# Another order and another spacing of the work that is laid between the steps of layer 0's attention

## The chip, the cores and the metric

The kernel runs on one core of one Trainium2 chip. The metric is the device time of one execution in microseconds (us). All arithmetic is in 32-bit floats.

## What is computed

The reference runs a first block of two layers and then a second block. The change touches layer 0 of the first block alone. Its parts that matter here are:

```python
shift, scale, gate = split(silu(c) @ w_ada[l] + b_ada[l], 3)       # the modulation, 6 x 512 columns of w_ada
h = x * (1 + scale) + shift                                        # 512 rows; the context's 256 rows likewise
(..., g_lat) = split(h @ w_in[l])                                  # the last 1024 columns of w_in are the gate
y_b = global_gqa(...)          # 4 heads, all keys
y_c = diff_attention(...)      # 4 heads, (softmax(q1 k1) - lam * softmax(q2 k2)) v
y_d = window_gqa_latent(...)   # 4 heads, keys within 128 positions, and the context
y = concatenate([y_a, y_b, y_c, y_d]) * silu(g_lat)
x_new = layer_norm(alpha * x + gate * (y @ w_out))
```

## The kernel before

The 512 + 256 rows stand as six tiles of 128 rows, four of the latent and two of the context (tiles 4 and 5). Five programs (one for each engine) are written out by hand, and each of them walks through the same steps in the same order; semaphores tie them together. The PSUM has eight banks of 128 x 512 floats.

**The attention of a layer** is `attend(l)`. In layer 0 it goes through 48 steps and four more that empty the pipeline, so i = 0 to 51. Steps 0 to 23 are the differential kind (c in the code: a tile and one of its four heads, with two score maps), 24 to 35 the global kind (b) and 36 to 47 the local kind (d), both with a tile and two heads a step. TensorE (PE) issues in step i: q, the transposes of a tile's queries, if step i + 2 starts a tile; S, the scores of step i (L973), into banks 2 to 5, which the two maps of every step share; t, the transposes of the softmax weights of step i - 2 (L988); V, the products with the values (L1007) of step i - 3, in the differential kind on even steps alone; o, the transposes of a finished tile's heads (L748), on odd steps. ScalarE (ACT) issues in a differential step: the copy of the first half of t out of its bank, the two exponentials of step i (L1571), and only then the copy of the second half of t. VectorE (DVE) issues the row maxima of step i (L2141), the settling of step i - 1 and, in the later kinds, its share of the copies. S of step i + 1 writes where the exponentials of step i have read.

q, t and o use banks 6 and 7 in turn, by a place that `turn_banks` works out. `open_bank(b)` makes PE wait until the last user of a bank has been read out.

**The work laid between the steps** is the generator `gate_and_ada(l)` of each engine, and `alongside` spreads it evenly over the 52 steps. It has 40 pieces in layer 0: first 24 pieces G, each two products of 128 x 512 of the gate's second half (`product_pieces`, L799), four to a tile, into bank 0, the fourth followed by ACT's copy (`gate`); then eight parts of the modulation (`ada`, `later_ada`: parts 4 and 5 of layer 0 and all six of layer 1), each of two pieces. The first, P, is eight products of 32 rows x 512 columns into bank 0 (L761), which ACT copies to a row in SBUF. The second, T, is four transposes of that row (L748) into bank 6 + n % 2, where n is the part's number in its layer; T opens that bank first, whoever used it last. DVE then reduces the bank (L1958) and adds the bias (L1960):

```python
bank_free(0, [ada_act.at("row", l, n)])
yield True
b = 6 + n % 2
open_bank(b)
pe.wait_ge(*ada_act.at("row", l, n))
transposes(raw[n % 2], 4, b).then_inc(turn_done(("ada", l, n)), 1)
```

A piece is issued after all that its step issues. With P and T numbered 0 to 7, the even spacing puts G on steps 0 to 29 (12 of them on steps 0 to 14, and 12 on steps 15 to 29), P0 on step 31, T0 on 32, P1 on 33, T1 on 35, P2 on 36, T2 on 37, P3 on 39, T3 on 40, P4 on 41, T4 on 42, P5 on 44, T5 on 45, P6 on 46, T6 on 48, P7 on 49 and T7 on 50. After step 51 comes the first tile of y, then a barrier of the engines and the layer's end, which needs the gate of all tiles and the modulation.

**Weights** come through a ring of six slots of 512 KB (`list_weights`, `Weights`). SyncE's queue (SP) issues the loads in the order of the list, each after the products of the block six places ahead of it have ended. A part of the modulation takes four loads (32 for the eight parts), the gate's second half four, and the output projection eight.

Of the kernel before, what the change touches and what calls it, by code (L numbers as in the profile page):

```python
# [23 lines left out]
DEPTH = 2  # L24
# [118 lines left out]
        pass  # L143


def run(stream):
    for _ in stream:
        pass
# [18 lines left out]
def later_ada(l):  # L167

    return [(l, 4), (l, 5)] + [(l + 1, n) for n in range(6)]


def list_weights(ring, a):
    def rows(key, w, c0, n, per=2, moved=()):
        v = w.rearrange("(k p) n -> p k n", p=P)
        for i in range(KT // per):
            ring.add(key + (i,), v[:, per * i:per * i + per, c0:c0 + n], (per, n), i in moved)

    def cols(key, w, c0, split=False):
        v = w.rearrange("(k p) n -> p k n", p=P)
        ring.add(key, v[:, :, c0:c0 + P], (KT, P), split)  # L180

    def wide(key, w, k):
        ring.add(key, w[k * P:(k + 1) * P, :].rearrange("p (k n) -> p k n", k=1), (1, D), True)

    for n in range(4):
        rows(("ada", 0, n), a["w_ada"][0], 512 * n, 512)
    for l in range(DEPTH):
        w = a["w_in"][l]
        for t in range(2):
            tag, c = (("b", C_B), ("d", C_D))[t]  # L190
            rows((tag, l), w, c, 512)
            for name, c in (("q", C_AQ), ("f", C_FF), ("b", C_FB)):
                cols(("hg", l, t, name), w, c + P * t)
            if t == 0:
                rows(("ai", l), w, C_AI, 256)
                rows(("c", l), w, C_C, 512)
            else:
                rows(("cv", l), w, C_CV, 256)
        rows(("g0", l), w, C_G, 512)
        rows(("g1", l), w, C_G + 512, 512)  # L200
        if l < DEPTH - 1:
            for l_, n in later_ada(l):
                rows(("ada", l_, n), a["w_ada"][l_], 512 * n, 512)
        for n in range(2):
            rows(("out%d" % n, l), a["w_out"][l], 512 * n, 512, 2, MOVED[l, n])
    w = a["w_in_2"][0]
    for i, c in enumerate(FM2[2:]):
        cols(("fm", i + 2), w, c)
    rows(("gmlp", 2), w, 0, 512)
    for i, c in enumerate(FM2[:2]):  # L210
        cols(("fm", i), w, c)
    rows(("q", 2), w, 512, 256, 4)
    rows(("kv", 2), w, 1024, 512)

    def compression(i):
        v = a["nsa_cmp_w1_2"][0, i].rearrange("(k p) e -> p k e", p=P)
        for half in range(2):
            ring.add(("w1", i, half), v[:, 8 * half:8 * half + 8, :], (8, CMP_HID))

    compression(0)  # L220
    rows(("ng", 2), w, 1536, P, 8)
    compression(1)
    for d in range(KT):
        for n in range(4):
            cols(("gate", d, n), a["w_gate_2"][0], n * D + d * P, True)
        cols(("branch", d), a["w_branch_2"][0].rearrange("n c d -> (n c) d"), d * P, True)
    for k in range(KT):
        wide(("out2", k), a["w_out_2"][0], k)
    for f in range(FT):
        cols(("mlp1", f), a["w_mlp1_2"][0], f * P, True)  # L230
    for f in range(FT):
        wide(("mlp2", f), a["w_mlp2_2"][0], f)


def build(nc, a, out):
    ctx = ExitStack()
    with ctx:
# [313 lines left out]
        def attention_steps(l):  # L551

            out_ = []
            if l == 2:
                for m in range(LT):
                    for kind in BRANCHES:
                        for e in range(2):
                            out_.append((kind, m, e))
                return out_
            for kind in "cbd":  # L560
                for m in range(last_q_of(l)):
                    for e in range(4 if kind == "c" else 2):
                        out_.append((kind, m, e))
            return out_

        def window(kind, m):
            if kind == "cmp":
# [157 lines left out]
        def tensor_program(pe):  # L725
# [207 lines left out]
                    bank_free(0, [gate_act.at("row", tag, l, m)])  # L933

            def gate_and_ada(l):
                yield from gate(l, 1)
                if l < DEPTH - 1:
                    yield from ada(later_ada(l))

            def prepare(l, k, banks):  # L940
                kind, m, e = attention_steps(l)[k]
# [161 lines left out]
            def layer(l):  # L1103
                for t in range(2):
                    beside = stream(l, t)
                    for m in range(AHEAD):
                        if t == 0 and l == 0 and m + 2 < TT:
                            modulate(0, m + 2, stage_x[m + 2])
                        next(beside)
                        if t == 0 and l > 0 and m == 0:  # L1110
                            pe.wait_ge(*tail_dve.at("z", l - 1, TT - 1))
                            modulate(l, TT - 1, z[:, TT - 1, :])
                    scan_inputs(l, t)
                    next(beside)
                    alongside(scan(l, t), 14, beside, beside_steps(l, t))
                    stage_end(1 + 3 * l + t)
                alongside(attend(l), len(attention_steps(l)) + 4, gate_and_ada(l), 4 * last_q_of(l) + (16 if l < DEPTH - 1 else 0))
                turn_y(l, 0)
                stage_end(3 + 3 * l)
                layer_end(l)  # L1120
# [271 lines left out]
        def scalar_program(act):  # L1392
# [154 lines left out]
                    yield True  # L1547

            def gate_and_ada(l):
                yield from gate(l, 1)  # L1550
                if l < DEPTH - 1:
                    yield from ada(later_ada(l))

            def prepare(l, k, banks):
                kind, m, e = attention_steps(l)[k]
# [105 lines left out]
            def layer(l):  # L1661
                for t in range(2):
                    beside = stream(l, t)
                    for m in range(AHEAD):
                        if t == 0 and l == 0 and m + 2 < TT:
                            modulate(0, m + 2)
                        next(beside)
                    scan_inputs(l, t)
                    if t == 0:
                        act.wait_ge(*lam_dve.at("sums", l))  # L1670
                        act.activation(lam[:, 2:4], lam[:, 0:2], ACT.Exp).then_inc(lam_act(("exp", l)), 1)
                    next(beside)
                    alongside(scan(l, t), 14, beside, beside_steps(l, t))
                    stage_end(1 + 3 * l + t)
                alongside(attend(l), len(attention_steps(l)) + 4, gate_and_ada(l), 4 * last_q_of(l) + (16 if l < DEPTH - 1 else 0))
                stage_end(3 + 3 * l)
                layer_end(l)

# [236 lines left out]
        def vector_program(dve):  # L1915
# [169 lines left out]
                    yield True  # L2085

            def gate_and_ada(l):
                for _ in range(4 * last_q_of(l)):
                    yield True
                if l < DEPTH - 1:  # L2090
                    yield from ada(later_ada(l))

            def settle(l, k):
                kind, m, e = attention_steps(l)[k]
# [246 lines left out]
            def layer(l):  # L2341
                lam_init = 0.8 - 0.6 * math.exp(-0.3 * l)
                dve.wait_ge(*gains.at("all", l))
                dve.tensor_scalar(neg_sinks[:], sinks[:], -1.0, None, ALU.mult).then_inc(lam_dve(), 1)
                dve.tensor_tensor(lam_rows[:, 0::2, :], lam_rows[:, 0::2, :], lam_rows[:, 1::2, :], ALU.mult).then_inc(lam_dve(), 1)
                dve.wait_ge(*lam_dve.now())
                dve.reduce_sum(lam[:, 0:2], lam_rows[:, 0::2, :], AX).then_inc(lam_dve(("sums", l)), 1)
                for t in range(2):
                    beside = stream(l, t)
                    for m in range(AHEAD):  # L2350
                        if t == 0 and l == 0 and m + 2 < TT:
                            modulate(0, m + 2)
                        next(beside)
                    scan_inputs(l, t)
                    next(beside)
                    alongside(scan(l, t), 14, beside, beside_steps(l, t))
                    if t == 0:
                        dve.wait_ge(*lam_act.at("exp", l))
                        dve.tensor_tensor(lam[:, 4:5], lam[:, 3:4], lam[:, 2:3], ALU.subtract).then_inc(lam_dve(), 1)
                        dve.wait_ge(*lam_dve.now())  # L2360
                        dve.tensor_scalar(lam[:, 5:6], lam[:, 4:5], -lam_init, None, ALU.add).then_inc(lam_dve(("lam", l)), 1)
                    stage_end(1 + 3 * l + t)
                alongside(attend(l), len(attention_steps(l)) + 4, gate_and_ada(l), 4 * last_q_of(l) + (16 if l < DEPTH - 1 else 0))
                stage_end(3 + 3 * l)
                layer_end(l)

# [455 lines left out]
```

## Time and profile before

| | us |
|---|---|
| median of 3 runs | 2188.32 (2186.58 to 2189.64) |
| the profiled execution, its own time | 2191.96 |
| its span on the core | 2190.1 |
| PE busy in the span | 2054.4 (94%) |
| VectorE busy | 1154.3 (53%) |
| ScalarE busy | 783.3 (36%) |

The sum of a change is made against the profiled execution; the time outside its span is 1.9 us. Rows of the trace give the start in us from the span's start, a duration, the engine, the line, and, in brackets, how long the engine had been idle and what ended that. A product of 32-bit floats stands as two records, a transpose as one. The rows themselves stand below.

### The profile page before, as it was taken

To read this page: it belongs to the slowest core of one execution; us is meant where nothing else is said; L and a number is where in the kernel's file an instruction comes from. 1 tells how busy PE (TensorE), PEld (TensorE's weight loads), DVE (VectorE), ACT (ScalarE), POOL (GpSimd) and SP (SyncE) were. 2 spreads that over 40 slices of the span, in tenths; PEclk is the share of its full clock that TensorE was granted. 3 is DMA by queue.
4 is the path that set the end of the run, shared out by engine and by line. 5 is a ranking of instruction groups with operands and counts; after the bars stand their busy time and mean duration, and the time that the engine had idled before them with its cause. 6 is when DMAs were issued, how large, how long until landed. Compare 5 with 4: busy or idle time off the path is not lost.

```text
span 2190.1 us, 27157 instructions
## 1 busy us (share of the span) xinstructions
PE 2054.4 (94%) x10380; PEld 1445.3 (66%) x10380; DVE 1154.3 (53%) x2484; ACT 783.3 (36%) x1671; POOL 54.5 (2%) x96
## 2 busy tenths in 40 slices
PE   5989999999889999898998989999999999999999
PEld 2565465555547665564565677885788877888887
DVE  1655136555657848226467677977444435333333
ACT  2132123554453323233465524336422224223222
POOL 2000000000000000000000010000000000000000
PEclk9999999999889999999799999998999999999999
DMA  9111010001444211121000332221233332333331
GB/s 294 35 52 39 25 63 20 20 1 40 154 154 122 78 48 39 40 64 62 1 1 11 107 81 77 79 78 29 68 97 97 98 94 60 98 99 91 97 97 66
DMA packets 152687, 157.32 MB, mean 72 GB/s; under 512 B 5676, under 2 KB 114384, under 8 KB 152560
## 3 DMA queue, kind: packets, MB, share of 16 engines
q1 hardware_dynamic: 146672, 137.91, 20.7%
q0 software_dynamic: 5888, 17.68, 2.8%
q8 instruction: 84, 1.38, 0.3%
q14 instruction: 43, 0.35, 0.1%
HBM read 151.37 MB, written 4.19 MB: 71 GB/s over the span
## 4 chain that ended last, share of the span: by engine, by line
PE 73%; DVE 16%; ACT 5%; issue 3%; DMA 2%; POOL 1%; ACTq 0%; PEldq 0%; DVEq 0%; SPq 0%; PEld 0%; POOLq 0%
PE psum L787 11%; PE psum L1280 10%; PE psum L1281 9%; PE psum L1282 9%; PE psum L973 6%; PE psum L799 5%; PE psum L815 5%; PE psum L988 3%; PE psum L1007 3%; PE psum L748 2%; DVE arena L2430 2%; DVE stats L2141 1%; ACT arena L1394 1%; PE psum L833 1%; PE psum L761 1%
## 5 line engine op out<-in xcount | busy, mean ns | idle before, releaser
L1394 ACT ACTIVATE arena<-psum 128x384 f32<-128x384 f32 (+5 forms) x510 | 199.9, 420 | 626.7 <-PE psum L748 171.1
L1280 PE MATMUL psum<-part,part 128*128 128x512 f32 x992 | 387.7, 391 | 5.2 <-DVE part L2545 2.7
L1281 PE MATMUL psum<-part,part 128*128 128x512 f32 x992 | 387.4, 391 | 0.0
L1282 PE MATMUL psum<-part,part 128*128 128x512 f32 x992 | 387.3, 390 | 0.0
L787 PE MATMUL psum<-arena 128*128 128x512 f32 (+1 forms) x960 | 319.4, 488 | 0.8 <-ACTq L1397 0.8
L1394 ACT ACTIVATE part<-arena 128x1024 fp32r<-128x1024 f32 (+1 forms) x214 | 190.6, 924 | 226.3 <-PE psum L1282 150.0
L2545 DVE TENSOR_TENSOR part<-arena,part 128x1024 fp32r<-128x1024 f32 x112 | 137.1, 1226 | 252.1 <-ACT part L1394 252.1
L787 PEld LDWEIGHTS psum<-arena 128*128 128x128 f32 x960 | 178.9, 190 | 120.7 <-issue 105.7
L2141 DVE TENSOR_REDUCE stats<-psum 128x1 f32<-128x768 f32 (+6 forms) x208 | 139.0, 709 | 153.1 <-PE psum L973 151.6
L1280 PEld LDWEIGHTS psum<-part,part 128*128 128x128 f32 x992 | 186.6, 188 | 45.9 <-DVE part L2545 3.1
L1282 PEld LDWEIGHTS psum<-part,part 128*128 128x128 f32 x992 | 186.7, 188 | 39.3
L1281 PEld LDWEIGHTS psum<-part,part 128*128 128x128 f32 x992 | 186.6, 188 | 38.9
L799 PE MATMUL psum<-arena 128*128 128x512 f32 x320 | 157.7, 623 | 3.4 <-ACT arena L1394 3.4
L973 PE MATMUL psum<-arena 64*128 64x256 f32 (+6 forms) x672 | 152.2, 506 | 8.9 <-ACT arena L1571 7.8
L1571 ACT ACTIVATE arena<-psum,stats 128x768 f32<-128x768 f32 (+6 forms) x208 | 144.8, 702 | 41.4 <-DVE stats L2109 19.9
L988 PE MATMUL psum<-ident,arena 128*128 128x128 f32 (+1 forms) x672 | 117.3, 304 | 13.0 <-DVE arena L2155 9.0
L973 PEld LDWEIGHTS psum<-arena 64*128 64x128 f32 (+1 forms) x672 | 72.3, 199 | 82.6 <-issue 56.7
L815 PE MATMUL psum<-arena 128*128 128x512 f32 (+1 forms) x352 | 119.4, 501 | 0.0
L988 PEld LDWEIGHTS psum<-ident,arena 128*128 128x128 f32 (+1 forms) x672 | 77.5, 149 | 62.6 <-issue 37.9
L748 PE MATMUL psum<-ident,arena 128*128 128x128 f32 x456 | 76.7, 289 | 40.4 <-ACT arena L1394 16.8
L815 PEld LDWEIGHTS psum<-arena 128*128 128x128 f32 x352 | 67.2, 192 | 51.6 <-issue 47.6
L1007 PE MATMUL psum<-arena 128*64 128x128 f32 (+1 forms) x1344 | 101.0, 297 | 0.0
(279 smaller groups left out, 2358.7 us busy)
## 6 DMA issues: line engine op xcount, KB each, us to landing
arena<-in_w_in SPq DMA_DIRECT2D x75, 512.0 KB, 4.1
arena<-in_w_mlp SPq DMA_DIRECT2D x64, 512.0 KB, 3.8
arena<-in_w_ada SPq DMA_DIRECT2D x48, 512.0 KB, 5.3
arena<-in_w_gate SPq DMA_DIRECT2D x32, 512.0 KB, 4.0
arena<-in_w_out SPq DMA_DIRECT2D x24, 512.0 KB, 3.9
arena<-in_w_in SPq DMA_DIRECT2D x16, 256.0 KB, 3.3
arena<-in_w_branch SPq DMA_DIRECT2D x8, 512.0 KB, 3.7
arena<-in_x POOLq DMA_DIRECT2D x4, 512.0 KB, 9.1
```

Of the source, the lines that this page charges most:

```text
L787: mm = pe.matmul(bank(b)[:, c0:c1], lhs[:, k, m * P:(m + 1) * P], ring.view(tag, l, k // 2)[:, k % 2, c0:c1], start=k == 0, stop=k == kt - 1)
L799: mm = pe.matmul(bank(b), lhs[:, k, m * P:(m + 1) * P], ring.view(tag, l, k // 2)[:, k % 2, :], start=k == 0, stop=k == KT - 1)
L815: mm = pe.matmul(bank(b)[:, 0:t1 - t0], ring.view("hg", l, t, name)[:, k, :], h_t[:, k, t0:t1], start=k == 0, stop=k == KT - 1)
L973: mm = pe.matmul(score_map(l, k, j)[:, c0:c0 + rhs.shape[-1]], q[r0:r1, at_q:at_q + P], rhs[r0:r1, :], start=True, stop=True)
L988: mm = pe.transpose(bank(b)[0:w, x * P:(x + 1) * P], weights_of(l, k)[:, j, c0:c0 + w], ident[:])
L1007: mm = pe.matmul(bank(b)[64 * j:64 * j + 64, u * P:(u + 1) * P], value(kind, s, h), head_turned(l, k_, i)[0:w, x * P:(x + 1) * P], start=x ...
L1280: pe.matmul(dst, lo, x_hi_, start=first, stop=False)
L1281: pe.matmul(dst, hi, x_lo_, start=False, stop=False)
L1282: return pe.matmul(dst, hi, x_hi_, start=False, stop=last)
L1394: return act.activation(dst, src, ACT.Copy)
L1571: act.activation(weights_of(l, k)[:, j, lo:hi], score_map(l, k, j)[:, lo:hi], ACT.Exp, bias=col[:, j:j + 1], scale=1.0, accum_out=col[:, 2 ...
L2141: dve.reduce_max(col[:, j:j + 1], score_map(l, k, j)[:, lo:hi], AX, negate=True).then_inc(soft_dve(*names), 1)
```

## The change

The generator `gate_and_ada` gives the modulation's 16 pieces first and the gate's 24 after them, on PE, ACT and DVE. The gate's four loads stand behind the modulation's 32 in the list. And `paced` with a list of counts takes the place of `alongside`:

```diff
+def paced(main, filler, counts):
+    for _, n in zip(main, counts):
+        for _ in range(n):
+            next(filler)
+    for _ in filler:
+        pass
...
         rows(("g0", l), w, C_G, 512)
-        rows(("g1", l), w, C_G + 512, 512)
         if l < DEPTH - 1:
             for l_, n in later_ada(l):
                 rows(("ada", l_, n), a["w_ada"][l_], 512 * n, 512)
+        rows(("g1", l), w, C_G + 512, 512)
...
+        def pieces_beside(l):
+            n = len(attention_steps(l)) + 4
+            if l < DEPTH - 1:
+                parts_ = {0: 1, 1: 2, 2: 2, 3: 2, 5: 2, 7: 2, 9: 2, 11: 2, 13: 2}
+                pieces = {15, 17, 19, 21, 23, 25, 27, 29, 31, 33} | set(range(36, 49))
+                return [parts_.get(i, 1 if i in pieces else 0) for i in range(n)]
+            else:
+                total = 4 * last_q_of(l) + (16 if l < DEPTH - 1 else 0)
+                upto = [-(-i * total // n) for i in range(n + 1)]
+                return [upto[i + 1] - upto[i] for i in range(n)]
...
             def gate_and_ada(l):
-                yield from gate(l, 1)
                 if l < DEPTH - 1:
                     yield from ada(later_ada(l))
+                yield from gate(l, 1)
...
-                alongside(attend(l), len(attention_steps(l)) + 4, gate_and_ada(l), 4 * last_q_of(l) + (16 if l < DEPTH - 1 else 0))
+                paced(attend(l), gate_and_ada(l), pieces_beside(l))
```

So in layer 0: P0 on step 0; T0 and P1 on step 1; T1 and P2 on 2; T2 and P3 on 3; then T3 and P4 on 5, T4 and P5 on 7, T5 and P6 on 9, T6 and P7 on 11, T7 and the first G on 13. The other 23 G: one on each odd step from 15 to 33 (ten), and one on each of steps 36 to 48 (thirteen). For layer 1 the counts are those of the even spacing. The bank of each T, and its user before, by `turn_banks`: T0 bank 6, the queries' transposes; T2 bank 6, the first half of t of its own step; T1, T3, T4, T5, T6 and T7 the bank of the second half of t of their own step.

## Rows read from the trace of the kernel before

**Rows 1.** Busy time by stretch: length, engines (instructions), PE clock, DMA share, GB/s

```profile
391.70:413.80 22.10, 22.10 (x101) 11.05 (x101) 13.71 (x22) 11.51 (x26) 0.00 (x0) 0.92 0.06 22
413.80:463.10 49.30, 48.80 (x304) 28.65 (x302) 32.62 (x53) 30.01 (x70) 0.00 (x0) 1.00 0.00 1
463.10:496.70 33.60, 32.36 (x175) 16.91 (x174) 17.11 (x48) 16.50 (x54) 0.00 (x0) 0.95 0.01 1
496.70:565.20 68.50, 64.70 (x488) 39.88 (x486) 41.39 (x99) 33.61 (x83) 0.00 (x0) 0.95 0.28 93
565.20:637.40 72.20, 60.51 (x444) 35.16 (x442) 44.78 (x148) 33.65 (x101) 0.00 (x0) 0.86 0.34 118
```

**Rows 2.** Timeline of PE: the scores of steps 5, 8, 9 and 15

```profile
413.76 2.18 PE L973 MATMUL psum<-arena 32*128 32x512 f32 x8
...
429.19 1.56 PE L973 MATMUL psum<-arena 32*128 32x512 f32 x8
...
432.95 2.37 PE L973 MATMUL psum<-arena 32*128 32x512 f32 x8
...
463.11 1.56 PE L973 MATMUL psum<-arena 32*128 32x512 f32 x8
```

**Rows 3.** Timeline of step 3: scores, the second exponential, then ACT's two copies

```profile
405.27 1.92 PE L973 MATMUL psum<-arena 32*128 32x512 f32 x8
...
408.97 0.90 ACT L1571 ACTIVATE arena<-psum,stats 128x768 f32<-128x768 f32 x1
...
409.84 0.99 ACT L1394 ACTIVATE arena<-psum 128x384 f32<-128x384 f32 x2
```

**Rows 4.** Timeline of PE: a G and a P

```profile
446.69 1.88 PE L799 MATMUL psum<-arena 128*128 128x512 f32 x4
...
544.98 1.92 PE L761 MATMUL psum<-arena,csil 128*32 128x512 f32 x16
```

**Rows 5.** Timeline of PE: o of step 41 with P4 behind it, and T4 of step 42

```profile
606.07 0.44 PE L748 MATMUL psum<-ident,arena 128*128 128x128 f32 x2 [1.44 <-ACT arena L1394]
606.44 1.92 PE L761 MATMUL psum<-arena,csil 128*32 128x512 f32 x16
...
614.25 0.66 PE L748 MATMUL psum<-ident,arena 128*128 128x128 f32 x4 [1.23 <-ACT arena L1394]
```

**Rows 6.** Busy time by stretch, as Rows 1, around two slow stretches of PE's clock

```profile
502.70:506.10 3.40, 1.97 (x10) 1.05 (x10) 1.89 (x3) 2.53 (x6) 0.00 (x0) 1.00 0.00 0
506.10:512.90 6.80, 6.80 (x28) 4.26 (x25) 3.01 (x5) 2.92 (x7) 0.00 (x0) 0.50 0.00 0
...
581.20:591.50 10.30, 9.42 (x47) 4.39 (x44) 5.48 (x16) 3.37 (x10) 0.00 (x0) 0.50 0.03 4
```

**Rows 7.** Timeline of PE: the scores of steps 21, 22, 30 and 31

```profile
486.11 0.70 PE L973 MATMUL psum<-arena 32*128 32x256 f32 x4
...
488.11 1.22 PE L973 MATMUL psum<-arena 32*128 32x256 f32 x4 [0.71 <-ACT arena L1571]
...
535.09 1.56 PE L973 MATMUL psum<-arena 64*128 64x512 f32 x8
...
539.65 1.56 PE L973 MATMUL psum<-arena 64*128 64x512 f32 x8
```

**Rows 8.** Timeline of PE: S of steps 38, 44 and 47; the last transposes of the attention

```profile
574.84 1.35 PE L973 MATMUL psum<-arena 64*128 64x384 f32 x8
...
621.41 0.70 PE L973 MATMUL psum<-arena 64*128 64x256 f32 x4
...
637.49 0.70 PE L973 MATMUL psum<-arena 64*128 64x256 f32 x4
...
652.26 1.31 PE L748 MATMUL psum<-ident,arena 128*128 128x128 f32 x10 [0.28 <-DVE ada_t L1958]
```

**Rows 9.** The page's DMA issues: the modulation's loads, KB each, median us to landing

```profile
arena<-in_w_ada SPq DMA_DIRECT2D x48, 512.0 KB, 5.3
```

**Rows 10.** Busy time by stretch, as Rows 1: the first 40 us, all loads

```profile
0.00:40.00 40.00, 18.41 (x94) 5.78 (x95) 3.65 (x20) 7.45 (x12) 10.80 (x24) 0.91 0.98 358
```

More of the change, by code:

```diff
@@ L1549, in gate_and_ada @@
             def gate_and_ada(l):
-                yield from gate(l, 1)
                 if l < DEPTH - 1:
                     yield from ada(later_ada(l))
+                yield from gate(l, 1)
             def prepare(l, k, banks):
@@ L1674, in layer @@
                     stage_end(1 + 3 * l + t)
-                alongside(attend(l), len(attention_steps(l)) + 4, gate_and_ada(l), 4 * last_q_of(l) + (16 if l < DEPTH - 1 else 0))
+                paced(attend(l), gate_and_ada(l), pieces_beside(l))
                 stage_end(3 + 3 * l)
@@ L2087, in gate_and_ada @@
             def gate_and_ada(l):
+                if l < DEPTH - 1:
+                    yield from ada(later_ada(l))
                 for _ in range(4 * last_q_of(l)):
                     yield True
-                if l < DEPTH - 1:
-                    yield from ada(later_ada(l))
             def settle(l, k):
@@ L2362, in layer @@
                     stage_end(1 + 3 * l + t)
-                alongside(attend(l), len(attention_steps(l)) + 4, gate_and_ada(l), 4 * last_q_of(l) + (16 if l < DEPTH - 1 else 0))
+                paced(attend(l), gate_and_ada(l), pieces_beside(l))
                 stage_end(3 + 3 * l)
```

## The prediction

> **What bounds the kernel now.** I read the busy time by stretch first, over layer 0's attention (391.7 to 654 us of 2190.1). From step 5 to step 14 PE is busy 48.80 of 49.30 us; from the start of the local kind (565.2) it is busy 60.51 of 72.20 us, at a mean granted clock of 0.86 [rows 1]. So the differential kind is full of PE work, pieces included, and the local kind has holes. VectorE and ScalarE are busy less than PE in every stretch: what ends a wait is the order of the steps, not an engine that is out of time.
>
> I then read the timeline for what a step must wait for. In step 3 the scores end at 407.19, the second exponential at 409.87, and ACT's copy of the second half of t stands behind it: two copies in 0.99 us from 409.84, so the first is done by about 410.3 [rows 3]. That is 3.2 us after the end of the scores. Steps 8 and 9 give the shortest distance of two steps' scores: 430.75 to 435.32, 4.57 us from end to end, in a step with V and no piece; the second S is drawn out to 2.37 us because it waits for the exponentials inside itself [rows 2]. A piece costs nothing only as far as it fits into that.
>
> **The size of the pieces.** G takes 1.9 us and P 1.9 us [rows 4]; T, four transposes, 0.6 us after its wait (614.25 to 614.84) [rows 5]. The change removes and adds no piece: 24 G and 8 of P and T are 65 us of PE work before and after. It moves them, so its whole effect is waits and clock.
>
> **Steps 0 to 14: longer.** This is where I expect the loss. T opens bank 6 or 7, and on steps 2, 5, 7, 9, 11 and 13 the bank's last user is the second half of t of the same step, whose copy ACT makes after both exponentials. No row of before has a T in this kind; the nearest are in the local kind, where o of step 41 waits 1.44 us and T4 of step 42 waits 1.23 us for an ACT copy, and P4, which needs nothing of that copy, starts only behind o at 606.44 [rows 5]. So P will queue behind T too. An odd step then is: 3.2 us from the end of S to T, 0.6 for T, 1.9 for P (or the first G), 1.56 for the next S, 7.3 from end to end. The even step behind it has no piece and keeps the 4.57. A pair is 11.9 us. Now ten steps, 5 to 14, take 463.11 - 413.76 = 49.35, so 9.9 a pair [rows 2]: five pairs lose 10, and the queries' transposes ahead of three even steps, now inside waits, add 0.9. Steps 0 to 4 become 5.0 + 4.5 + 7.6 + 4.9 + 4.5 = 26.5 (step 2 has a T that waits; step 3's T follows the first half, whose copy comes ahead of the exponentials) instead of 22.1 [rows 1], 4.4 more. Sum: **15.3 us slower**. The bounds: if the wait is there and costs all that it can, each of the six takes 3.2 us, 19; if ACT's copy came at once, only the first steps' shift of 1 or 2 us would be left.
>
> The ScalarE copies of eight rows, VectorE's eight pairs of small operations and the bias additions move with the parts. ACT's row copy (0.6 us) falls beside the next S, and DVE's reduction comes after its row maxima and settling, over 1 us before the next t wants the bank; both are covered, and without the cover the price is 0.6 us a part, 5 in all.
>
> **Steps 15 to 35: shorter.** Two G (12 before, 10 after), P0, P1, T0 and T1 leave: 4 x 1.9 + 2 x 0.6 = 8.8 us. Most is real: steps without a piece go down to 2.0 us where 256 columns are scored (steps 21 to 22) and to 4.56 in the global kind, with no wait of PE shown (steps 30 to 31) [rows 7]. A piece on step 25 also fills the hole of 502.7 to 506.1, in which PE is busy 1.97 of 3.40 us at full clock and after which it runs 6.8 us at 0.50 [rows 6]. The two slow stretches here are 10.2 us long (clock 0.95 over 102 us [rows 1]), worth 5. Sum **14 us faster**, the clock put at full for now.
>
> **Steps 36 to the end: a little shorter.** Six P and six T leave (15) and thirteen G come (24.7), 9.7 more PE work. On even steps G lies beside the exponentials. On odd steps o waits for them (the 1.44 of [rows 5]), the piece is behind o and so is added whole. A pair of steps 38 to 43 comes to 6.6 + 8.2 = 14.8 us; now three pairs take 621.41 - 574.84 = 46.6 [rows 8], 15.5 each: 2 less. The steps beside them come out 1 less. At the end T6, P7 and T7 stand on steps 48 to 50, and nothing but G is left on 48: from S of step 47 (637.49) to the last transposes (652.26, waiting for the modulation's DVE addition) it is 14.8 us [rows 8], and 4 leave. Sum **7 us faster**, at full clock again.
>
> **The clock.** PE's two levels are 2.4 GHz (1.00) and 1.2 GHz (0.50). Where PE had been busy 1.97 of 3.40 us it fell [rows 6]; steps 5 to 14 with 48.80 of 49.30 kept 1.00 [rows 1]. Each of the waiting T leaves a hole of about 2.4 us with short work around it. I put four falls there, of 3.4 us each, which is half of 6.8, at a loss of 1.7: 7. For what is left of slow clock later I put back 4 in steps 15 to 35 and 3 in the local kind, which keeps the waits ahead of o. Ends: no loss at all, and a fall at each of six waits at 2.6 us plus 8 later, 24.
>
> A rule speaks against the change here. The Trainium skill (TensorE: Matmul & The Clock Gate, A second HAM failure mode: psum-queue depth-cycling) says that small idle gaps between groups of matmuls, from cycling through PSUM banks, make the clock swing between its levels. By it each of the six waits would bring a fall, and the sum would be some 4 us higher, about 2201; the wait of 1.44 at 606.07 brought none [rows 5]: P4 behind it takes 1.92, as at full clock, so the sum goes by four.
>
> **The loads.** The 32 loads of the modulation move from 381 to 640 us into 377 to 450. P0 to P3 come on four steps running, 2 MB each. The first 40 us moved 358 GB/s [rows 10], 5.9 us for 2 MB, and the median landing is 5.3 us [rows 9]; steps 2 and 3 are 12.5 us long together, so the six slots keep up, and I put nothing. If landings take twice the median, three parts wait up to 3 us: 8. The gate's loads have ample time, two of the eight output loads come early and the rest as G leaves its slots, at step 45 and later, no later than now.
>
> **Sum.** 15.3 + 7 - 14 + 4 - 7 + 3 = 8.3 us slower, against the profiled execution 2191.96, so 2200.3. That execution is 3.6 above the median, 2188.32; against the median it is **2197 us**.
>
> **Rivals.**
> - *The later kinds win (faster), 0.25.* With G on every step the holes ahead of o no longer bring slow stretches, and the waits at T bring few. Then the clock terms vanish: 15.3 - 14 - 7 = 6 faster, and 10 if even steps hide more of S's own wait: 2180 to 2184. It decides if the clock's loss stays under 4 us. For it: the 0.86 of the local kind, some 20 us at half clock [rows 1], of which 10.3 in one piece [rows 6]. Against it: the holes ahead of o stay, since G comes after o.
> - *The clock falls at every wait (slower still), 0.12.* 24 in place of 14 of clock: 2207, and up to 2213 if the falls last two stretches. The fall after 506.1 speaks for it [rows 6], the wait at 606.07 without one against it [rows 5].
> - *Loads come late, 0.08.* The 8 us above: 2205. P1's second half is the place, five us after P0. Against it, the rate [rows 10].
> - *It does nothing that shows, 0.17.* The loss at T and the gain in the later kinds cancel, 2184 to 2192.7. A measurement tells about 0.2%, 4.4 us.
>
> **How the numbers follow.** The forecast has 0.38, within 2193 to 2202. With the rivals on its side slower has 0.58, the same 0.17, faster 0.25. The range takes in the faster case's 2180 and the clock's 2212 and leaves out what lies past them.
>
> **What would show it.** In the profile after: a wait of 2 to 2.5 us of PE ahead of L748, put down to ACT's copy, on steps 2, 5, 7, 9, 11 and 13, P behind it; the scores of step 5 about 4 us later, those of step 15 about 20 later than 463.11; some four falls of the clock between; then the distance shrinking to about 10 by step 36, and about 8 at the barrier. Wrong would be: T without a wait in the differential kind; PE at full clock through the local kind; waits of L761 for DMA; or a difference after the barrier.

## The result and the profile after

| | before | changed |
|---|---|---|
| median of 10 runs each, us | 2184.8 (2182.43 to 2190.35) | 2195.29 (2186.75 to 2206.72) |
| profiled execution, its own time | 2191.96 | 2195.09 |
| its span | 2190.1 | 2193.2 |

The ratio is 1.0048, with a 95% interval of 1.0034 to 1.0063: the changed kernel is slower by some 10.5 us, about half a per cent. With seven more runs of before, its median came to lie 3.5 us under the one that the prediction was made against.

The two profiled executions differ by only 3.1 us. The busy time by stretch shows where. Of the changed kernel, in the columns of [rows 1]: the scores of step 0 to those of step 5, to step 15, to step 36, to the layer's end, and all that follows:

```profile
391.20:418.86 27.66, 24.87 (x161) 10.25 (x161) 14.21 (x27) 13.51 (x29) 0.00 (x0) 0.88 0.80 281
418.86:488.57 69.71, 58.59 (x360) 29.22 (x359) 33.94 (x63) 30.86 (x70) 0.00 (x0) 0.83 0.41 137
488.57:577.39 88.82, 85.07 (x614) 52.02 (x612) 57.44 (x142) 49.62 (x137) 0.00 (x0) 0.98 0.00 1
577.39:661.80 84.41, 72.12 (x462) 41.32 (x461) 49.56 (x156) 41.51 (x121) 0.00 (x0) 0.96 0.08 26
661.80:2193.20 1531.40, 1455.27 (x7279) 1098.35 (x7279) 830.36 (x1703) 544.28 (x1076) 31.32 (x54) 0.98 0.24 71
```

And of the kernel before, the whole attention and what follows:

```profile
391.70:654.05 262.35, 241.17 (x1590) 138.72 (x1591) 155.42 (x387) 134.67 (x354) 0.00 (x0) 0.92 0.21 71
654.05:2190.10 1536.05, 1461.32 (x7279) 1101.77 (x7279) 830.74 (x1703) 544.67 (x1076) 31.37 (x54) 0.98 0.24 71
```

The attention takes 270.6 us instead of 262.35, 8.3 more (its first scores come 0.5 us earlier, so its end lies 7.75 us later). The stretch behind it has the same 7279 PE records and no edit, and takes 1536.05 in one execution and 1531.40 in the other; PE is busy 6 us less, and its clock is at 1.2 GHz for 71.6 us of it in the one and for 54.8 in the other. So a profiled execution's end says less here than its stretches, and the runs' medians say more than one execution's end.

| stretch | before | changed | difference |
|---|---|---|---|
| steps 0 to 4 | 22.1 | 27.7 | +5.6 |
| steps 5 to 14 | 49.35 | 69.7 | +20.4 |
| steps 15 to 35 | 102.1 | 88.8 | -13.3 |
| steps 36 to the layer's end | 88.8 | 84.4 | -4.4 |

What fills the 20.4 us stands in the timeline of PE of the changed kernel, steps 5 to 8 (start, duration; in brackets the idle time before it and what ended that). L995 is the scores, L770 T or o, L783 P, L1010 t, L1029 V, L971 the queries' transposes:

```profile
418.86 2.37 PE L995 MATMUL psum<-arena 32*128 32x512 f32 x8
421.15 0.88 PE L1010 MATMUL psum<-ident,arena 128*128 128x128 f32 x6
424.43 1.11 PE L770 MATMUL psum<-ident,arena 128*128 128x128 f32 x4 [2.40 <-ACT arena L1416]
425.47 3.64 PE L783 MATMUL psum<-arena,csil 128*32 128x512 f32 x16
429.05 0.69 PE L971 MATMUL psum<-ident,arena 128*128 128x128 f32 x2
429.66 1.91 PE L995 MATMUL psum<-arena 32*128 32x512 f32 x8
...
437.20 0.44 PE L770 MATMUL psum<-ident,arena 128*128 128x128 f32 x2 [0.25 <-ACT arena L1416]
439.35 0.66 PE L770 MATMUL psum<-ident,arena 128*128 128x128 f32 x4 [1.71 <-ACT arena L1416]
439.94 2.99 PE L783 MATMUL psum<-arena,csil 128*32 128x512 f32 x16
```

T3 waits 2.40 us on step 5 for ACT's copy, and T4 on step 7 waits 1.71 behind an o that itself stood in the hole. The other waits are 2.53 (step 2), 2.40 (9), 1.71 (11) and 2.40 (13), 13.2 us in all. P behind the wait takes 3.64 us where [rows 4] have 1.92. The copy that ends T3's wait is the last of ACT's step, which the timeline of ACT shows:

```profile
421.74 0.49 ACT L1416 ACTIVATE arena<-psum 128x384 f32<-128x384 f32 x1 [1.74 <-PE psum L1010]
422.13 0.90 ACT L1593 ACTIVATE arena<-psum,stats 128x768 f32<-128x768 f32 x1
422.91 0.20 ACT L1593 ACTIVATION_READ_ACCUMULATOR arena<-psum,stats 128x1 f32 x1
423.00 0.90 ACT L1593 ACTIVATE arena<-psum,stats 128x768 f32<-128x768 f32 x1
423.79 0.21 ACT L1593 ACTIVATION_READ_ACCUMULATOR arena<-psum,stats 128x1 f32 x1
423.88 0.50 ACT L1416 ACTIVATE arena<-psum 128x384 f32<-128x384 f32 x1
```

The first half of t is copied at 421.74, the two exponentials follow, and the second half at 423.88 to 424.38; T starts at 424.43, 3.2 us after the scores ended, as in [rows 3]. And the clock, in the stretches at the six waits, T1's first (PE clock is the third number from the end):

```profile
406.50:409.90 3.40, 3.40 (x17) 0.59 (x16) 0.36 (x2) 0.00 (x0) 0.00 (x0) 0.50 0.53 183
423.60:430.40 6.80, 5.97 (x24) 2.10 (x26) 0.80 (x3) 1.72 (x5) 0.00 (x0) 0.50 0.26 71
440.70:444.10 3.40, 3.40 (x16) 0.95 (x10) 0.00 (x0) 0.60 (x1) 0.00 (x0) 0.51 0.50 113
450.90:457.70 6.80, 4.93 (x22) 1.60 (x22) 1.95 (x7) 1.97 (x6) 0.00 (x0) 0.50 0.10 18
468.00:471.40 3.40, 3.40 (x18) 0.55 (x10) 0.28 (x2) 0.00 (x0) 0.00 (x0) 0.50 0.20 26
481.60:485.00 3.40, 3.40 (x8) 1.42 (x8) 0.13 (x1) 0.25 (x1) 0.00 (x0) 0.50 0.00 0
```

PE runs at 1.2 GHz in all of them. Such a fall came with each of the six waits, within it or up to 1.4 us after its end: those of steps 5 and 9 last 6.8 us, the others 3.4, 27.3 us in all. Later in the attention there are three of 3.4 us (at 522.6, 601.1 and 618.1), where the kernel before has seven with 37.5 us from 489 on. Both executions have 41 us of slow clock in the attention; it has moved from the later steps to the early ones.

### The profile page after: what moved, and what is told of

Same layout as the page of the kernel before. It is cut to its first block, busy times and chain, and to the rows that moved or that the text cites. A ratio compares the mean times of both kernels' runs of the same rounds, so it can differ in the third digit from the quotient of the medians.

```text
span 2193.2 us, 27158 instructions
## 1 busy us (share of the span) xinstructions
PE 2049.0 (93%) x10380; PEld 1435.9 (65%) x10380; DVE 1153.7 (53%) x2484; ACT 783.7 (36%) x1671; POOL 54.0 (2%) x96
## 4 chain that ended last, share of the span: by engine, by line
PE 73%; DVE 16%; ACT 5%; issue 3%; DMA 2%; POOL 1%; DVEq 0%; PEldq 0%; ACTq 0%; PEld 0%; POOLq 0%
PE psum L809 11%; PE psum L1302 10%; PE psum L1304 9%; PE psum L1303 9%; PE psum L995 6%; PE psum L821 5%; PE psum L837 5%; PE psum L1010 3%; PE psum L1029 3%; PE psum L770 2%; DVE arena L2452 2%; PE psum L783 1%; DVE stats L2163 1%; ACT arena L1593 1%; ACT arena L1416 1%
## 5 line engine op out<-in xcount | busy, mean ns | idle before, releaser
L995 PE MATMUL psum<-arena 64*128 64x256 f32 (+6 forms) x672 | 149.0, 497 | 8.5 <-ACT arena L1593 7.4
L770 PE MATMUL psum<-ident,arena 128*128 128x128 f32 x456 | 78.1, 292 | 51.7 <-ACT arena L1416 29.7
L1010 PE MATMUL psum<-ident,arena 128*128 128x128 f32 (+1 forms) x672 | 112.7, 294 | 13.2 <-DVE arena L2177 11.5
L995 PEld LDWEIGHTS psum<-arena 64*128 64x128 f32 (+1 forms) x672 | 69.0, 196 | 83.2 <-issue 55.6
L1010 PEld LDWEIGHTS psum<-ident,arena 128*128 128x128 f32 (+1 forms) x672 | 74.5, 144 | 62.1 <-issue 37.5
L770 PEld LDWEIGHTS psum<-ident,arena 128*128 128x128 f32 x456 | 53.8, 147 | 83.9 <-ACT arena L1416 37.1
```

The source lines that it names most:

```text
L770: mm = pe.transpose(bank(b)[0:width, i * P:(i + 1) * P], src[:, i * width:(i + 1) * width], ident[:])
L995: mm = pe.matmul(score_map(l, k, j)[:, c0:c0 + rhs.shape[-1]], q[r0:r1, at_q:at_q + P], rhs[r0:r1, :], start=True, stop=True)
L1010: mm = pe.transpose(bank(b)[0:w, x * P:(x + 1) * P], weights_of(l, k)[:, j, c0:c0 + w], ident[:])
```

## The experiments

Theory A is the prediction's: T opens a bank whose last reader is a late copy, P queues behind it, and the hole lets the clock fall. The rivals are that the clock is no cost, that loads or ACT's queue are the cause and T only shows it, and that it is the spacing or the order as such. Each kernel starts from the changed one. The ratios are to the kernel before, run on the same chip beside it.

**The holes filled (e1_filled).** Eight products of no use ahead of each waiting T.

```diff
+        HOLES = ((0, 5), (1, 1), (1, 2), (1, 3), (1, 4), (1, 5))
...
                     b = 6 + n % 2
+                    if (l, n) in HOLES:
+                        open_bank(0)
+                        keep_going(0, 8)
                     open_bank(b)
```

> The changed kernel with eight extra products of 128 x 128 (about 2.0 us) into bank 0 ahead of each of the six T that wait. They depend on nothing that T waits for. Theory A (two costs: the wait itself, about 13 us in all, and the clock that falls after each hole): PE's waits ahead of T shrink to 0.5 us or less, each odd step keeps its length apart from the clock, no fall of the clock is left between steps 2 and 15, the scores of steps 5 and 15 come to stand about 60 us apart instead of 69.7, and the kernel is 8 to 12 us faster than the changed one, that is within 0.2% of the one before. Theory B (the clock falls are no cost, only the wait is): PE's time from step 5 to 15 stays at 69 to 70 us and the kernel stays 0.4 to 0.5% slower than before.

Ratio 0.9999 (0.9983 to 1.0015), median 2183.7 us. Steps 5 to 14, in the columns of [rows 1]:

```profile
417.14:476.80 59.66, 57.31 (x441) 35.89 (x439) 33.94 (x63) 30.79 (x70) 0.00 (x0) 1.00 0.46 159
```

and T3 and T5 in the timeline of PE:

```profile
422.71 0.66 PE L772 MATMUL psum<-ident,arena 128*128 128x128 f32 x4 [0.61 <-ACT arena L1421]
...
446.61 0.66 PE L772 MATMUL psum<-ident,arena 128*128 128x128 f32 x4 [0.61 <-ACT arena L1421]
```

T still starts when the copy is done; only the clock is different, 1.00 instead of 0.83, and the ten steps take 59.7 us instead of 69.7. That splits the loss in this stretch: 10 us are the clock (69.71 - 59.66), and 10.3 are what the waits cost (59.66 - 49.35). The 10.3 is net of the pieces: these steps now hold four P, five T and one G where they held eight G, some 2.7 us less work. Theory A holds, with 0.6 to 0.7 us of wait where it said 0.5 or less. Products of no use bring the whole of the 0.48% back, by the clock alone: the waits stay as long as they were.

**P ahead of T (e2_p_first).** On PE, the two pieces of a step change places.

```diff
-                for l, n in parts_:
+                products(*parts_[0])
+                yield True
+                for p in range(1, len(parts_)):
+                    products(*parts_[p])
+                    yield True
+                    turned(*parts_[p - 1])
+                    yield True
+                turned(*parts_[-1])
+                yield True
```

> The changed kernel with P ahead of T wherever both stand on one step, on PE alone; nothing else moves. Theory A (T waits for the copy of the second half of t, and P queues behind it for nothing): P fills 1.9 us of the hole, the wait ahead of T falls from 1.7 to 2.5 us to about 0.5, steps 5 to 15 take about 51 us instead of 69.7, no fall of the clock there, and the kernel is 18 to 22 us faster than the changed one, 0.4 to 0.6% faster than before. Theory B (what lengthens the steps is the modulation's loads or the queue of ScalarE, and T only shows it): P is late too, and less than 5 us comes back.

Ratio 0.9972 (0.9956 to 0.9989), median 2179.2 us. Steps 5 to 14 take 53.8 us, not 51, and the gain over the changed kernel, by the two ratios, is some 17 us, not 18 to 22. The timeline of PE has the reason:

```profile
423.46 0.66 PE L770 MATMUL psum<-ident,arena 128*128 128x128 f32 x4 [0.55 <-ACT arena L1432]
...
463.70 0.84 PE L770 MATMUL psum<-ident,arena 128*128 128x128 f32 x4 [2.40 <-ACT arena L1432]
```

T3 (423.46) waits 0.55 us, as expected. But T7 on step 13 (463.70) stands with the first G, which the edit leaves behind it; it waits the full 2.40 and brings the one fall of the clock of these steps, at 464.0. The expectation had overlooked that. Theory B (loads or ACT) falls: P was late because of T.

**T in the first half's bank (e3_first_bank).** For T1, T3, T5 and T7 alone.

```diff
+        ADA_BANK = {(0, 5): 6, (1, 1): 6, (1, 3): 6, (1, 5): 6}
+
+        def ada_bank(l, n):
+            return ADA_BANK.get((l, n), 6 + n % 2)
...
-                    b = 6 + n % 2
+                    b = ada_bank(l, n)
```

> The changed kernel with T1, T3, T5 and T7 written into bank 6, where the first half of t of their step stands, instead of bank 7; T4 and T6 stay. Theory A: those four wait 0.25 us as T2 does, T4 and T6 keep 1.7 us and one fall of the clock each; 4 x 2.2 of wait and about 5 of clock come back, so 13 to 16 us against the changed kernel, 0.2 to 0.4% faster than before. Theory B (a wait of the same length shows up at the next t or at the exponentials, since the step cannot be shorter): under 4 us comes back.

Ratio 0.9979 (0.9964 to 0.9994), median 2178.92 us, some 15 us under the changed kernel. T3, T4, T5 and T6 in the timeline of PE:

```profile
420.83 0.66 PE L775 MATMUL psum<-ident,arena 128*128 128x128 f32 x4 [0.25 <-ACT arena L1421]
...
432.96 0.66 PE L775 MATMUL psum<-ident,arena 128*128 128x128 f32 x4 [1.71 <-ACT arena L1421]
...
442.59 0.66 PE L775 MATMUL psum<-ident,arena 128*128 128x128 f32 x4 [0.25 <-ACT arena L1421]
...
454.73 1.11 PE L775 MATMUL psum<-ident,arena 128*128 128x128 f32 x4 [1.71 <-ACT arena L1421]
```

The four whose bank changed wait 0.25 us, the two left alone 1.71. Of those two, T6's hole brought a fall (1.11 us for T) and T4's did not (0.66), where in the changed kernel both did. Nothing else was touched, so the bank, and with it the copy that frees it, is shown to be the cause of these waits.

**The order alone (e4_even).** Modulation first, at the even spacing of before.

```diff
-                parts_ = {0: 1, 1: 2, 2: 2, 3: 2, 5: 2, 7: 2, 9: 2, 11: 2, 13: 2}
-                pieces = {15, 17, 19, 21, 23, 25, 27, 29, 31, 33} | set(range(36, 49))
-                return [parts_.get(i, 1 if i in pieces else 0) for i in range(n)]
+                upto = [-(-i * 40 // n) for i in range(n + 1)]
+                return [upto[i + 1] - upto[i] for i in range(n)]
```

> The order of the change (modulation first) at the even spacing of before. T1, T2, T3, T4 wait for the copy of the second half of t (2.4, about 0.9 behind V, 2.4 and 1.7 us), T5 and T6 stand in the first half's bank, T7 (step 19) behind o. Theory A: waits of 7 to 8 us in all and three falls of the clock, so 6 to 10 us lost in steps 0 to 19, and some of it given back in the local kind, where no G stands on steps 38, 43 and 47: within 0.3% of before on either side, and 0.2 to 0.6% faster than the changed kernel. Theory B (the order alone is what costs): as slow as the changed kernel.

Ratio 1.0036 (1.0020 to 1.0053), median 2191.46 us: more than the 0.3% that was allowed, and 0.12% under the changed kernel, less than the 0.2 expected. The two intervals overlap, so these times alone leave theory B standing. The waits of T1 to T4 are 2.53, 1.08, 2.40 and 1.90 us, as foretold to 0.2; but the clock is slow for 27.3 us between 398 and 464, two stretches of 6.8 and one of 10.2 among them, not three short ones. Most of the change's loss comes with the order already, where T falls on a bank whose reader is late. It isn't the order as such: two kernels below have the same order and are faster than before.

**The spacing alone (e5_gate_first).** The gate first, as before, at the counts of the change.

```diff
             def gate_and_ada(l):
+                yield from gate(l, 1)
                 if l < DEPTH - 1:
                     yield from ada(later_ada(l))
-                yield from gate(l, 1)
```

(and the same on ACT and DVE and in the list of weights)

> The spacing of the change with the order of before: the gate's 24 pieces first, then the modulation, at the counts of the changed kernel (two G on odd steps to 13, G to step 27, P0 on 29, T7 on 48). It tells order from spacing. Theory A (the loss is the T among the differential steps): no T there, so no wait of PE ahead of L770 of over 0.5 us before step 29, steps 5 to 15 take 53 to 56 us (six to seven G more than before at 1.9 us, less what the holes take), later steps give it back; the whole is within 0.3% of before. Theory B (the spacing alone, nothing on even steps, costs it): slower than before by 0.4% or more.

Ratio 1.0017 (0.9999 to 1.0035), median 2189.62 us: within the 0.3%, and perhaps slower than before. Steps 5 to 14 take 57.9 us, over the 53 to 56, at a clock of 1.00. No T waits there, but G does:

```profile
424.95 1.98 PE L821 MATMUL psum<-arena 128*128 128x512 f32 x4 [1.22 <-ACT arena L1416]
...
447.88 1.98 PE L821 MATMUL psum<-arena 128*128 128x512 f32 x4 [1.17 <-ACT arena L1416]
```

Two G on one step cross from one tile to the next, and the second needs bank 0, which ACT copies only behind its exponentials. That is the same trap on another bank, which the expectation had missed. It had miscounted the pieces too: these steps hold ten G where before had eight, not six or seven more. The two make 3.8 of the 8.5 us, and three waits (the third at 470.81, 1.17 us) 3.6. By the medians the spacing alone costs a third of what the change does; the interval takes in nothing and most of it.

**T on even steps (e6_t_even).** P on steps 0, 1 and the odd ones from 3 to 13, T on step 1 and the even ones from 2 to 14, each T in the bank of its step's first half.

```diff
-                parts_ = {0: 1, 1: 2, 2: 2, 3: 2, 5: 2, 7: 2, 9: 2, 11: 2, 13: 2}
-                pieces = {15, 17, 19, 21, 23, 25, 27, 29, 31, 33} | set(range(36, 49))
+                parts_ = {0: 1, 1: 2, 2: 1, 3: 1, 4: 1, 5: 1, 6: 1, 7: 1, 8: 1, 9: 1, 10: 1, 11: 1, 12: 1, 13: 1, 14: 1}
+                pieces = {15, 17, 19, 21, 23, 25, 27, 29, 31, 33, 35} | set(range(36, 49))
...
+        ADA_BANK = {(0, 5): 6, (1, 0): 6, (1, 1): 7, (1, 2): 6, (1, 3): 7, (1, 4): 6, (1, 5): 7}
```

> The changed kernel with P on steps 0, 1 and the odd steps 3 to 13, and T on step 1 and the even steps 2 to 14, each T in the bank of the first half of t of its step; the first G moves to step 15 and one G to step 35. Theory A (the loss was T behind a late copy, with P behind it): no wait ahead of T of over 0.3 us, every step near the 4.57 us that the scores need, steps 5 to 15 in 46 to 48 us (before 49.35, changed 69.7), no fall of the clock there; 0.5 to 0.8% faster than before. Theory B (the differential steps have no room for the modulation, wherever it stands; its loads or DVE's reductions come late): steps 5 to 15 take 52 us or more and it is no faster than the kernel with P ahead of T (0.28% under before).

Ratio 0.9925 (0.9908 to 0.9943), median 2167.46 us, against 2183.38 for before beside it: faster than both kernels. Steps 5 to 14:

```profile
415.07:460.92 45.85, 45.34 (x371) 27.26 (x370) 33.27 (x64) 30.83 (x70) 0.00 (x0) 1.00 0.67 232
```

45.9 us with five P and five T among them, against 49.35 with eight G before [rows 2]. The loads move 232 GB/s here, and PE is busy 45.34 of 45.85 us, so they hold nothing up. The differential steps have room for the modulation, and theory B falls.

**The same by counts alone (e8_counts).** The counts of the last kernel without its table of banks.

> The changed kernel with other counts and nothing else: P and T at the steps of e6_t_even, G too, and every T in the bank that the change gives it. By the places of the banks T2 to T7 then fall on the first half's bank by themselves, and T1 alone waits for the second half. Theory A (the place of T against the banks in turn is the whole loss): one wait of 2.4 to 2.6 us ahead of T on step 2, none over 0.3 after it up to step 19, steps 5 to 15 in 46 us, and within 0.2% of e6_t_even, 0.6 to 0.8% faster than before. Theory B (the table of banks in e6_t_even was needed): waits of 1.7 to 2.4 us remain and less than half of its gain.

Ratio 0.9946 (0.9928 to 0.9964), median 2172.04 us: 0.54% where 0.6 was the least expected, 0.21% over the kernel with the table. The only wait over 0.3 us ahead of T up to step 19 is T1's:

```profile
406.27 0.66 PE L770 MATMUL psum<-ident,arena 128*128 128x128 f32 x4 [2.52 <-ACT arena L1416]
...
430.53 0.44 PE L770 MATMUL psum<-ident,arena 128*128 128x128 f32 x2 [0.25 <-ACT arena L1416]
```

It brings 6.8 us of slow clock at 407.0, and the scores of step 5 come at 418.62 instead of 415.07, 3.6 us later; steps 5 to 14 take 46.0. Theory A holds, a little short of its sizes: other counts, with T2 to T7 one step later and P2 to P7 one or two, turn a loss of half a per cent into a gain of the same size. These counts also put P and T on different steps, so the gain isn't the bank's alone; what the bank costs by itself stands under e3_first_bank. What the 0.21% says beyond T1 lies within the intervals.

**o behind G (e7_o_late).** As the kernel with T on even steps, and from step 24 on PE issues the piece first and the heads' transposes after it.

```diff
-                    if 0 <= i - 4 < len(steps_) and steps_[i - 4][2] == last_e(steps_[i - 4][0]):
+                    ends = 0 <= i - 4 < len(steps_) and steps_[i - 4][2] == last_e(steps_[i - 4][0])
+                    if ends and not (l == 0 and i >= 24):
                         turn_heads(l, i - 4, banks)
                     yield True
+                    if ends and l == 0 and i >= 24:
+                        turn_heads(l, i - 4, banks)
```

> As e6_t_even, and from step 24 on PE issues o behind the piece of its step instead of ahead of it. Theory A (in the later kinds a G behind o is added whole, as the prediction says): PE's waits of 1.2 to 1.7 us ahead of o on steps 39, 41, 43 and 45 are filled by G, each of these steps is 1.2 to 1.7 us shorter, a fall or two of the clock go; 5 to 9 us under e6_t_even. Theory B (o only moves its wait to the scores behind it, which need the same exponentials): under 1.5 us.

Ratio 0.9914 (0.9894 to 0.9933), median 2165.37 us, which can't be told from 0.9925. In the timeline of PE, G and o of step 39 and the second half of t and G of step 40:

```profile
570.64 1.88 PE L826 MATMUL psum<-arena 128*128 128x512 f32 x4
572.50 0.44 PE L775 MATMUL psum<-ident,arena 128*128 128x128 f32 x2
...
578.35 0.63 PE L1015 MATMUL psum<-ident,arena 128*128 128x128 f32 x2 [1.72 <-DVE arena L2185]
578.78 3.42 PE L826 MATMUL psum<-arena 128*128 128x512 f32 x4
```

o waits no more, and step 39 takes 7.2 us from scores to scores (565.89 to 573.08) instead of 8.9. But the next step's t then waits 1.72 us for DVE instead of 1.18, the clock falls there (3.42 us for G), and step 40 takes 9.1 us instead of 6.8. The local kind's gain moves on to the next wait; neither theory had that, and B is nearer.

**Fewer G in the local kind (e9_thin_local).** As the kernel by counts alone, with six G of the local kind's odd steps on steps 16 to 26.

```diff
-                pieces = {15, 17, 19, 21, 23, 25, 27, 29, 31, 33, 35} | set(range(36, 49))
+                pieces = {15, 17, 19, 21, 23, 25, 27, 29, 31, 33, 35} | {16, 18, 20, 22, 24, 26} | set(range(36, 49, 2))
```

> As e8_counts, with the G of the local kind's odd steps (37, 39, 41, 43, 45 and 47) moved to steps 16, 18, 20, 22, 24 and 26. Theory A (a G behind o is added whole, and so is one on these full steps, but without G the holes of the local kind bring PE's clock down more often): the six steps lose what the odd ones gain, two or three more falls of the clock in the local kind, 3 to 6 us slower than e8_counts. Theory B (thirteen G in the local kind fill holes that nothing else fills): 8 us slower or more. Theory C (it makes no difference where they stand): within 2 us.

Ratio 0.9948 (0.9936 to 0.9960), median 2174.27 us beside 2172.04. B falls. In the profiled executions the layer's end comes at 641.1 instead of 635.9, with 13.6 us of slow clock in the local kind against 3.4, which is A's mechanism. But the one is the slowest of its six runs and the other the fastest, and the medians tell 2.2 us, inside the intervals. Between A and C it stays open. Where six of the thirteen G stand makes no difference that shows.

## Why the prediction was right, and where its sizes were off

It was right in the sign, the place and the mechanism, and near in the size: 0.48% in the runs, 10.5 us, against the 0.40%, 8.7 us, by which 2197 is over 2188.32. That 2195.29 stands so close to 2197 owes something to the kernel before, whose median came out 3.5 us lower. On the profiled executions' stretches it is 8.3 us, as foretold, and that match is luck. Steps 0 to 14 with their clock cost 26.0 where 15.3 + 7 stood, 3.7 more; the later steps gave 17.7 where 14 stood, 3.7 more. By its own steps:

- *The bank wait in the differential kind* was right in place, cause and length. Foretold: 2 to 2.5 us on six named steps. Measured: 2.53, 2.40, 1.71, 2.40, 1.71, 2.40. The two short ones have o in the hole, which the prediction did not take into account. Without the clock, in the kernel with the holes filled, they cost 10.3 us in steps 5 to 14 against 10.9 foretold, and a pair of steps takes 11.9 us, as foretold.
- *P behind T* was right: with P ahead, steps 5 to 14 go from 69.7 to 53.8 us, the clock's part included.
- *Steps 0 to 4*: 5.6 us against 4.4; T1's fall of the clock is in it.
- *The clock's term* is the one that was mis-sized. It was put at four falls of 3.4 us and 7 us; there were six, two of them of 6.8, and filling the holes of steps 5 to 14 alone gave 10.0 us back. The Trainium skill (TensorE: Matmul & The Clock Gate, A second HAM failure mode: psum-queue depth-cycling) had it that gaps of this kind swing the clock, and the trace of the changed kernel agrees with it at every one of the six. Four was put instead of six because the wait of 1.44 us at 606.07 had brought no fall. But [rows 5] hold a second wait, T4's of 1.23 us at 614.25, and in the kernel before the clock fell right behind it (the row below this list). The prediction read the one witness and not the other. Nor does the length of a hole alone tell: this one of 1.23 us has a fall behind it, one of 1.71 us in the kernel with the four banks changed has none, nor have three of about 1.2 us in steps 5 to 14 of the kernel with the spacing alone. What decides stays open.
- *Steps 15 to 35*: 13.3 us gained against 10 (14 less 4 for the clock). One fall of 3.4 us was left there where two stretches, 10.2 us together, had been. The piece on step 25 filled the hole ahead of step 26's scores, as foretold (1.43 us idle before, none now). But step 24 had a G before and has none now, so step 25's scores wait 1.17 us, and the one fall is there, at 522.6. It is 1.7 us lost where 4 were put back, which is most of the 3.3 by which this term is off.
- *The local kind and the end*: 4.4 gained against 4, and its clock term of 3 was near too. The slow clock went from 27.3 us to 6.8, which at half speed is 3.4 lost. By the prediction's count PE has 9.7 us more work there, yet PE is busy 72.12 us against 73.22, so the faster clock paid for the added G.

The kernel before, in the columns of [rows 1], 1.1 us after its T4 began:

```profile
615.40:618.80 3.40, 3.40 (x23) 2.42 (x21) 2.19 (x7) 0.71 (x2) 0.00 (x0) 0.50 0.00 0
```

Too little loss in the first steps and too little gain in the later ones cancelled, and the sum came out better than its terms. The loads had next to no part: PE waited 0.4 us for them, a wait that the prediction had named as a sign of being wrong. Its last such sign, a difference after the barrier, came too (4.7 us less), with no edit there to cause it. The rival in which the later kinds win, at 0.25, needed two things. The first nearly came: from 489 on, 10.2 us of slow clock are left of 37.5. The second, waits at T that bring few falls, did not: the clock's loss had to stay under 4 us and was 10 in steps 5 to 14 alone. The rival at 0.12, a fall at every wait, was right in its mechanism and too high in its sum, since the later steps gave more.

## What to carry to other kernels

Before a filler is moved beside another loop, look up for each of its steps which buffer it opens and which instruction of which engine frees that buffer in the new place; in an engine that works in order, the price is the wait and all that queues behind it, and here also a slower clock for what comes next. When two resources alternate, shifting the filler by a step can be worth more than spreading it well: with T2 to T7 on the next step and P apart from T, the same pieces went from a loss of 0.48% to a gain of 0.54%. And if a hole can't be avoided, try what is independent first, P ahead of T.

## What the runs showed of the hardware that was not expected

PE's granted clock fell to 1.2 GHz in or behind six holes of 1.7 to 2.5 us, one in each of six steps of 9 to 11 us. Eight products in each, which compute nothing, kept it at 2.4 GHz for the 59.7 us from step 5 to 14 and saved 10 us. The stretch behind the attention, with the same instructions in both, took 1536.05 and 1531.40 us in two executions with PE busy 1461.32 and 1455.27, and 1529.88 in the kernel with T on even steps, at 71.6, 54.8 and 54.4 us of slow clock; so some 6 us of a profiled execution's time go with the clock, far from the edit. The changed kernel's ten runs spread over 20 us, those of before beside them over 8. The runs' mean granted clocks go with it: 0.982 in the changed kernel's fastest run (2186.75), 0.971 in its slowest (2206.72), and in between the clock never rises as the time grows. Which falls differ from run to run, no trace shows.
